# The input projection, the compression and both mixers of a transformer kernel laid out as one block on Trainium2

## The reference, cut to what matters

```python
a = rmsnorm(h, mix_norm[i])
proj = a @ w_in[i]
(hg_q, hg_f, hg_i, hg_g, n_q, n_kc, n_vc, n_ks, n_vs, n_kw, n_vw, n_gate) = jnp.split(proj, SPLIT_POINTS, axis=-1)
o_hg = hgrn2_mixer(hg_q, hg_f, hg_i, hg_g, lb_table[i], hg_out_norm[i])
o_nsa = nsa_mixer(n_q, n_kc, n_vc, n_ks, n_vs, n_kw, n_vw, n_gate, ...)
mixed = jnp.concatenate([o_hg, o_nsa], axis=-1).astype(h.dtype)
h = h + mixed @ w_out[i]
```

## Time and profile before

| | us |
|---|---|
| runs of the kernel before | 2066.91, 2068.8, 2072.6 |
| median | 2068.8 |
| the profiled execution: its own time | 2070.71 |
| its span in the trace | 2068.9 |
| PE busy in the span | 1998.7 |
| end of the last product of the projection | 98.4 |
| first instruction of the mixers on PE | 102.45 |
| last instruction of the mixers on DVE ends | 164.34 |
| first product of the output projection | 165.65 |

### The profile page before, as it was taken

One profiled execution on the slowest core, in us unless ns is written; L12 is line 12 of the kernel. 1 busy time (PEld: TensorE's weight loads), 2 busy tenths in 40 slices (PEclk: granted clock), 3 DMA queues, 4 the chain that ended last, 5 costly groups with the idle time before them and its releaser, 6 DMA issues. The chain is left out here.

```text
span 2068.9 us, 33672 instructions
## 1 busy us (share of the span) xinstructions
PE 1998.7 (97%) x13538; PEld 1761.6 (85%) x13538; DVE 1452.3 (70%) x2212; ACT 1058.8 (51%) x1977; POOL 34.5 (2%) x33
## 2 busy tenths in 40 slices
PE   8978999999999999999989999999999999998998
PEld 7868999999999888888877867877778888778998
DVE  7766599988898678888587757577764227667554
ACT  5664444467776555445573256452223217555444
POOL 0000000000000000000010000100000001000000
PEclk9989999999999999999999999999999999999999
DMA  6404556554444677777546420235673333124663
GB/s 240 150 1 130 176 184 186 190 166 135 146 138 145 197 253 262 257 254 251 163 133 206 161 72 17 92 133 186 240 280 108 102 99 101 32 73 154 194 190 126
DMA packets 94827, 326.90 MB, mean 158 GB/s; under 512 B 10321, under 2 KB 15825, under 8 KB 94673
## 3 DMA queue, kind: packets, MB, share of 16 engines
q1 hardware_dynamic: 94672, 324.75, 48.4%
HBM read 323.66 MB, written 1.05 MB: 157 GB/s over the span
## 5 line engine op out<-in xcount | busy, mean ns | idle before, releaser
L330 DVE TENSOR_TENSOR wlo<-raw,whi 128x1024 fp32r<-128x1024 f32 (+1 forms) x502 | 613.3, 1224 | 334.8 <-ACT whi L324 331.6
L324 ACT ACTIVATE whi<-raw 128x1024 fp32r<-128x1024 f32 (+1 forms) x502 | 525.4, 1049 | 378.2 <-PE ps L705 365.6
L703 PE MATMUL ps<-x_hi,whi 128*128 128x512 f32 (+1 forms) x976 | 333.1, 341 | 12.6 <-DVE x_lo L506 8.2
L704 PE MATMUL ps<-x_lo,whi 128*128 128x512 f32 (+1 forms) x976 | 329.1, 337 | 0.0
L705 PE MATMUL ps<-x_hi,wlo 128*128 128x512 f32 (+1 forms) x976 | 328.9, 337 | 0.0
L703 PE MATMUL ps<-xT_hi,whi 128*128 128x256 f32 x1136 | 324.7, 286 | 3.2 <-DVE xT_lo L504 2.9
L704 PE MATMUL ps<-xT_lo,whi 128*128 128x256 f32 x1136 | 318.3, 280 | 0.0
L705 PE MATMUL ps<-xT_hi,wlo 128*128 128x256 f32 x1136 | 316.7, 279 | 0.0
L703 PEld LDWEIGHTS ps<-x_hi,whi 128*128 128x128 f32 x976 | 183.4, 188 | 45.0 <-issue 14.3
L703 PEld LDWEIGHTS ps<-xT_hi,whi 128*128 128x128 f32 x1136 | 214.3, 189 | 3.5 <-issue 3.5
L704 PEld LDWEIGHTS ps<-xT_lo,whi 128*128 128x128 f32 x1136 | 214.5, 189 | 0.0
(11 more groups left out here) (435 smaller groups left out, 3311.5 us busy)
## 6 DMA issues: line engine op xcount, KB each, us to landing
raw<-peer_u_t SPq DMA_DIRECT2D x128, 512.0 KB, 3.5
raw<-peer_v_t SPq DMA_DIRECT2D x128, 512.0 KB, 4.0
raw<-ffn_in_t SPq DMA_DIRECT2D x88, 512.0 KB, 4.4
x<-ada_t SPq DMA_DIRECT2D x64, 512.0 KB, 4.5
raw<-ffn_out_t SPq DMA_DIRECT2D x44, 512.0 KB, 3.7
raw<-qkv_t SPq DMA_DIRECT2D x36, 512.0 KB, 4.1
gated<-ada_t SPq DMA_DIRECT2D x32, 512.0 KB, 5.7
raw<-w_in_t SPq DMA_DIRECT2D x24, 512.0 KB, 3.8
```

Of the source, the lines that this page charges most:

```text
L324: act.activation(whi[:, n % SPLIT, 0:w], raw[:, g % RAW, 0:w], ACT.Copy).then_inc(hi_done, 1)
L330: dve.tensor_tensor(wlo[:, n % SPLIT, 0:w], raw[:, g % RAW, 0:w], whi[:, n % SPLIT, 0:w].bitcast(F32), ALU.subtract).then_inc(lo_done, 1)
L703: pe.matmul(place, wh, xh, start=start, stop=False, skip_group_check=shared)
L704: pe.matmul(place, wh, xl, start=False, stop=False, skip_group_check=shared)
```

## The change

It has six parts.

1. **Order of the tiles.** The weights are packed, and taken, in another order: keys, forget logits, queries `nqk`, `qs`, the tall tile of 280, `gate`, and the tall tile of 512 (`hg_v`) last.
2. **Queries without norm.** The queries stay as the projection gives them. Eight small matmuls (L1326, two columns each) sum their squares by token; the root (`q_root`), its inverse (`q_rstd`) and root times slope (`q_slope`) are columns of one number per token. `bias` takes the slope from `q_slope`, then multiplies the maxima with `q_rstd` (L1558, one more DVE instruction per step); the exponentials take `q_rstd` as their scale, a pointer operand beside the bias, which was one already. The query gain goes into the gains of the keys. `compare_begin` gets one more multiplication.
3. **Tangents.** Silu, Sigmoid (but the first use of it and the forget logits) and the gelu are written with Tanh: `twice_silu` is one Tanh on ACT and one multiplication on DVE from PSUM, and the factor 2 goes into later constants. The order of ACT's instructions holds 14 table loads in this stretch before and 8 after.
4. **Decays and compression under earlier pieces.** `CMP_AT` goes from 13, 16, 19, 22 to 10, 11, 12, 13; the scan, the decays and the compression's second half come at w = 12 to 20; the compressed scores, which were part of the mixers, come at w = 21 to 24. The roots of the key heads, the query sums and the compressed keys come together at w = 18, their reciprocals and what follows at w = 18 and 19.
5. **One block.** The mixers' code becomes methods `end` that run behind w = 28 in the same block; `hg_turn` (the transpositions of `hg_begin`) runs behind piece 26 and `scores(0)` behind piece 27. The scores lie in banks 4 and 5. SBUF for the mixers is taken before the projection.
6. **Order of the end.** `hg_state(2)` stands behind `scores(5)`, `hg_give(0)` ahead of `scores(6)`, `hg_give(1)` ahead of `scores(7)`; before, they stood ahead of `scores(3)`, `scores(4)` and `scores(5)`.

Cut to its core:

```diff
-CMP_AT = [13 + 3 * m for m in range(2 * CMP_LEN * 64 // 1024)]
+CMP_AT = [10 + m for m in range(2 * CMP_LEN * 64 // 1024)]
...
-            def pe(self, pe, w):
-                if w == 5:
-                    pe.wait_ge(kon_loaded, 16)
-                    pe.wait_ge(heads_squared, 1)
-                    pe.matmul(ps[:, 4, :], k("ones64"), hn[:, 4:6, :].rearrange("p c t -> p (c t)"), start=True, stop=True).then_inc(heads_summed, 1)
-                if w == 9:
-                    pe.wait_ge(heads_squared, 2)
-                    for g in range(2):
-                        mm = pe.matmul(ps[:, 5 + g, :], k("ones64"), hn[:, 2 * g:2 * g + 2, :].rearrange("p c t -> p (c t)"), start=True, stop=True)
-                    mm.then_inc(heads_summed, 1)
-                if w in CMP_AT:
-                    self.window(pe, CMP_AT.index(w))
...
+                if w == 7:
+                    pe.wait_ge(kon_loaded, 16)
+                    pe.wait_ge(heads_squared, 1)
+                    pe.matmul(ps[:, 4, :], k("ones64"), hn[:, :, :].rearrange("p c t -> p (c t)"), start=True, stop=True).then_inc(heads_summed, 1)
...
+                if w == 15:
+                    pe.wait_ge(heads_squared, 2)
+                    for qb in range(TB):
+                        for c in range(NSA_G):
+                            at = 2 * (NSA_G * qb + c)
+                            mm = pe.matmul(ps[:, 6, at:at + 2], qsq[:, c, qb * P:qb * P + P], k("ones64", 0, P).rearrange("p (h n) -> p h n", h=2)[:, :, 0],
+                                           start=True, stop=True)
+                    mm.then_inc(heads_summed, 1)
...
+                if w == 17:
+                    pe.wait_ge(cmp_squared, 1)
+                    pe.matmul(ps[:, 5, 96:96 + N_CMP], k("ones64"), csq[:, :], start=True, stop=True).then_inc(cmp_summed, 1)
+                if w == 21:
+                    pe.wait_ge(values_spread, 1)
+                    pe.wait_ge(act_evacuated.h, act_evacuated.at(4))
+                    self.compare(pe)
+                if w == 26:
+                    self.hg_turn(pe)
+                if w == 27:
+                    self.scores(pe, 0)
+                if w == 28:
+                    self.end(pe)
+            def end(self, pe):
+                self.hg_scores(pe)
+                self.scores(pe, 1)
+                pe.wait_ge(act_evacuated.h, act_evacuated.at(10))
+                pe.wait_ge(dve_evacuated.h, dve_evacuated.at(8))
+                self.hg_state(pe, 0)
+                self.hg_state(pe, 1)
+                self.scores(pe, 2)
+                self.turn(pe, 0)
+                self.scores(pe, 3)
+                self.turn(pe, 1)
+                self.attend(pe, 0)
+                self.scores(pe, 4)
+                self.turn(pe, 2)
+                self.attend(pe, 1)
+                self.scores(pe, 5)
+                self.hg_state(pe, 2)
+                self.turn(pe, 3)
+                self.turn_compared(pe)
+                self.attend(pe, 2)
+                self.hg_give(pe, 0)
+                self.scores(pe, 6)
+                self.turn(pe, 4)
+                self.attend(pe, 3)
+                self.attend_compared(pe, 1)
+                self.hg_give(pe, 1)
+                self.scores(pe, 7)
+                self.turn(pe, 5)
+                self.attend(pe, 4)
...
+                for n in range(4):
+                    act.activation(part(pr[:, i % 3, :], i, n), part(sc[:, i % 2, :], i, n), ACT.Exp, bias=nm[:, i % 2, n:n + 1],
+                                   scale=qrstd[:, qb, c, n // 2:n // 2 + 1], accum_out=sums[:, i % 3, n:n + 1]).then_inc(nsa_exp, 1)
...
+                if w == 17:
+                    act.activation(tcond[:, :], v("cond", 0, 2 * C), ACT.Tanh, scale=0.5).then_inc(halved, 1)
+                    act.wait_ge(compressed, 1)
+                    act.activation(csq[:, :], ps[:, 5, 64:64 + N_CMP], ACT.Square).then_inc(cmp_squared, 1)
+                if w == 18:
+                    act.wait_ge(heads_summed, 2)
+                    act.activation(hn[:, :, :].rearrange("p c t -> p (c t)"), ps[:, 4, :], ACT.Sqrt, bias=eps[:, :], scale=1.0 / 64).then_inc(heads_root, 1)
+                    act.activation(flat(qroot), ps[:, 6, 0:2 * TB * NSA_G], ACT.Sqrt, bias=eps[:, :], scale=1.0 / 64).then_inc(heads_root, 1)
+                    act.wait_ge(cmp_summed, 1)
+                    act.activation(csq[:, :], ps[:, 5, 96:96 + N_CMP], ACT.Sqrt, bias=eps[:, :], scale=1.0 / 64).then_inc(cmp_root, 1)
...
+                    ins = dve.scalar_tensor_tensor(out=sc[:, i % 2, half * w:half * w + w].rearrange("p (a t) -> p a t", a=2),
+                                                   in0=dist[:, qb:qb + 1, 0:SEEN[i]].broadcast_to([P, 2, SEEN[i]]), scalar=qslope[:, qb, c, half:half + 1],
+                                                   in1=ps[:, SCORE_BANK + half, 0:w].rearrange("p (a t) -> p a t", a=2), op0=ALU.mult, op1=ALU.add)
+                ins.then_inc(nsa_biased, 1)
...
+                low = nm[:, i % 2, :].rearrange("p (h a) -> p h a", h=2)
+                dve.tensor_tensor(low, low, qrstd[:, qb, c, :].unsqueeze(2).broadcast_to([P, 2, 2]), ALU.mult).then_inc(nsa_max, 1)
+
...
+                if w == 18:
+                    dve.wait_ge(halved, 3)
+                    dve.tensor_scalar(tcond[:, :], tcond[:, :], 0.5, 0.5, ALU.mult, ALU.add).then_inc(curved, 1)
+                    dve.wait_ge(heads_root, 1)
+                    dve.reciprocal(hn[:, 0, :], hn[:, 0, :]).then_inc(heads_rstd, 1)
+                    dve.wait_ge(curved, 3)
+                    dve.tensor_tensor(v("cond", 0, 2 * C), v("cond", 0, 2 * C), tcond[:, :], ALU.mult)
+                    self.key_head(dve, 0)
+                if w == 19:
+                    dve.reciprocal(hn[:, 1, :], hn[:, 1, :]).then_inc(heads_rstd, 1)
+                    dve.wait_ge(heads_root, 2)
+                    dve.reciprocal(flat(qrstd), flat(qroot)).then_inc(heads_rstd, 1)
+                    dve.tensor_tensor(flat(qslope), flat(qroot), mk("slopes"), ALU.mult).then_inc(heads_rstd, 1)
+                    self.key_head(dve, 1)
+                    dve.wait_ge(cmp_root, 1)
+                    dve.reciprocal(crs[:, :], csq[:, :]).then_inc(heads_rstd, 1)
+                    dve.wait_ge(heads_rstd, 5)
+                    dve.scalar_tensor_tensor(out=kcn[:, :], in0=ps[:, 5, 64:64 + N_CMP], scalar=v("nsa_k", 0), in1=crs[:, :], op0=ALU.mult, op1=ALU.mult).then_inc(kcn_done, 1)
+                    dve.tensor_tensor(vblk[:, :, :], ps[:, 5, P:2 * P].unsqueeze(1).broadcast_to([P, NSA_G, P]),
+                                      k("rows").unsqueeze(2).broadcast_to([P, NSA_G, P]), ALU.mult).then_inc(values_spread, 1)
...
+        def twice_silu(n, dst):
+
+            return ("wide", n * P, slice(0, T), lambda act, place: act.activation(dst, place, ACT.Tanh, scale=0.5),
+                    lambda dve, place: dve.scalar_tensor_tensor(out=dst, in0=dst, scalar=1.0, in1=place, op0=ALU.add, op1=ALU.mult))
...
         product_stage(at_in, aH, [
             (4, 2, 512, [first(0), both(1, pair_of(cin, 0), ACT.Copy), first(2), dve_both(3, pair_of(nqk, 4))]),
+            (4, 2, 512, [first(0), both(1, pair_of(sig, 0), ACT.Sigmoid), first(2), both(3, pair_of(sig, 2), ACT.Sigmoid)]),
             (4, 2, 512, [first(0), both(1, pair_of(nqk, 0), ACT.Copy), first(2), dve_both(3, pair_of(nqk, 2))]),
-            (4, 2, 512, [first(0), both(1, pair_of(sig, 0), ACT.Sigmoid), first(2), both(3, pair_of(sig, 2), ACT.Sigmoid)]),
-            (4, 2, 512, [first(0), both(1, pair_of(qs, 0), ACT.Silu), first(2), both(3, pair_of(qs, 2), ACT.Silu)]),
-            (4, 2, 280, tall_n), (4, 2, 512, tall_v),
-            (4, 2, 512, [first(0), both(1, pair_of(gate, 0), ACT.Silu), first(2), both(3, pair_of(gate, 2), ACT.Silu)])],
+            (4, 2, 512, [first(0), twice_silu(1, pair_of(qs, 0)), first(2), twice_silu(3, pair_of(qs, 2))]),
+            (4, 2, 280, tall_n),
+            (4, 2, 512, [first(0), twice_silu(1, pair_of(gate, 0)), first(2), twice_silu(3, pair_of(gate, 2))]),
+            (4, 2, 512, tall_v)],
```

972 lines of the change are left out of this document (467 added, 505 removed).

## The result

The changed kernel takes **2076.68 us** (median of 8 runs, 2074.9 to 2080.81), the kernel before 2067.84 (8 runs, 2066.79 to 2072.6). The ratio is 1.0038, with a 95% interval of 1.0029 to 1.0047: 8.8 us slower by the medians and 7.9 by the ratio, which compares all runs; both are beyond the 6.2 us that the prediction named as the least that can be told from no change. Predicted were 2075.8, in a range of 2064 to 2085, with 0.52 on slower. Its profiled execution took 2076.37 us, with a span of 2074.6.

The account below looks back on a forecast made before the run. PE, busy 97% of the span, was taken to bound the kernel, with the mixers a chain over three engines. Terms 4.0 + 2.0 + 1.1 + 1.2 - 1.3 = +7.0 us on 2068.8 gave 2075.8, range 2064 to 2085.

Parts of the forecast that it names:

- Step 1, the projection: Projection: PE waits 2.35 and 2.95 us for late splits at pieces 19 and 20; with moved work, `bias(0)` starts 4.0 later.
- Step 2, the clock in the projection: Projection behind those waits: some 5 us of products run at half speed, +2.0 us taken.
- Step 1, what the one block is worth: End of the projection: the barrier's 2.40 us is saved, contained in the +4.0 by which `bias(0)` starts later.
- Step 3, the order of the mixers: Mixers from `bias(0)` on, at full clock: 5.7 us won up to `bias(5)`, 6.8 given back, +1.1.
- Step 4, the pointers: Mixers' 32 exponentials: a second pointer operand costs 0.04 us each, +1.2 us, bounds 0 to 2.2.
- Step 5, the low stretch that goes: Start of the mixers: the low-clock stretch up to 108 us goes, -1.3 us; the other 5.0 of low stretches stays.
- the first: Rival: PE never waits at pieces 19 and 20, total -0.3 us, 2068.5, no difference; chance 0.20.
- The clock did not stay up: Rival judged: clock at 1.00 through the mixers to the end, -6.5 us, 2062.3; chance 0.10.
- fall so much more often: Rival: clock falls again and again in projection and mixers, three further stretches add 6.0, +13 us, 2081.8; chance 0.20.

Follow-up runs that it names:

- x1_spread: Changed kernel with the DVE steps of w = 18 and 19 drawn apart and the compressed keys' square behind piece 18: 2070.92 us, +0.8 to the kernel before.
- x2: Changed kernel with `hg_state(2)` and both `hg_give` back where the kernel before has them in the mixers: 2074.49 us, +4.4 to before.
- x3: Changed kernel without the exponentials' scale pointer, `bias` slope a constant, queries' norm left out of the scores: 2072.56 us, +2.4 to before.
- y2: Changed kernel with only the mixers' order exchanged for a third one, scores one step further ahead: 2059.56 us, -9.2 to before.
- y3: Changed kernel with 16 idle transpositions ahead of the waits of `turn(0)`, `turn(2)`, `turn(6)` and 8 ahead of `turn_compared`: 2077.49 us, +8.8 to before.
- x7_spread_late_start: `x1_spread` with `hg_turn` and `scores(0)` behind the last piece, ACT's `hg_copies` moved from w = 27 to 28: 2071.76 us, +2.4 to before.
- The three experiments: Old order of the end on the changed kernel (2074.49 us) and on `x1_spread` (2071.1); new order of the end on the kernel before (2070.5).
- both experiments: Changed kernel without the second pointers (2072.56 us); kernel before with a pointer to ones as the exponentials' scale (2069.8 us).
- x6: `x1_spread` with a third order of the mixers, scores one step further ahead of `turn` and `attend`: 2054.82 us, -14.5 to before.
- y4_before_pointer: Kernel before with a pointer to a column of ones as scale of the 32 exponentials: 2069.8 us, +1.1 to before.

## Why the prediction was right, and where it was not

**Step 1, the projection: right in mechanism and size.** Forecast was PE waiting 2.35 and 2.95 us near 74 and 78; it waited 2.33 and 1.91, and the second one 2.64 at full clock. The root ended at 74.0 where 73.7 was laid out. Undoing the bunching took 8.0 us off the difference of medians, 6.2 by the ratios (`x1_spread`).

**Step 2, the clock behind the stalls: right.** +2.0 was taken from the row at 100 us; the granted clock was 0.73 and 0.50 from 76 to 84 us, and `bias(0)` came 6.0 us later, the sum of the two terms. `x1_spread` gave back 6.2. That the sum fits to a tenth is in part luck: the stretch behaves differently in each execution, and the four traces that hold the changed kernel's projection under another name (`x2`, `x3`, `y2`, `y3`) have `bias(0)` at 108.5, 110.2, 110.0 and 110.5.

**Step 1, what the one block is worth: the size right, the reason loose.** The sum had the barrier's 2.40 as saved and eaten by moved work. `x7_spread_late_start` shows the more exact reason: ACT's copies stand ahead of the last two splits and wait 4.92 us, so that what PE saves DVE loses.

**Step 3, the order of the mixers: +1.1 within what was found.** The three experiments put it at 0 to 3. The offsets laid out for full clock (22.2 for `bias(5)`, 30.4, 36.0) came as 26.3, 36.7 and 42.6; those of the kernel before (27.9, 33.8, 36.9) are 30.8, 36.8 and 40.0 in its trace. So the lead that the new order wins up to `bias(5)` and gives back came as forecast in kind, 4.5, 0.1 and -2.6 us where 5.7, 3.4 and 0.9 were laid out. The layout at full clock held none of the low stretches; that they make the whole difference is not shown.

**Step 4, the pointers: the term that was mis-sized.** I took 0.04 us for each exponential, below the 0.07 of the nearest row, and nothing for `bias`, whose slope becomes a pointer as well. Measured were 0.09 and, per `bias`, 0.12 for the pair. That is 3.0 + 1.0 us on the engines where 1.2 stood; how much of it reached the total is not shown (on the kernel before 1.1 us for the 3.0, in an interval from nothing to all of it). The Trainium skill, "ScalarE: Activation LUTs", section "What ACT_TABLE_LOAD costs", has about 93 ns for each [128,1] pointer operand; the traces of the changed kernel and of both experiments agree with it (0.585 against 0.49), and the page was nearer than my reading of one row.

**Step 5, the low stretch that goes: half right.** It went (1.00 at 108 to 116 us), but the others grew: in windows of 2 us the granted clock is 0.71 or less at 118 to 126, 132 to 136, 142 to 146 and 156 to 164 us, and before at 102 to 108, 114 to 118, 124 to 128 and 148 to 158. Over the mixers it is 0.83 in both. So the gain of 1.3 doesn't show, and step 4 was too small as well. Both would take the mixers over the forecast +1.0; together they would make more than the +2.0 of the trace, and no experiment parts them: the same mixers took 61.8, 62.9 and 62.0 us in the traces of the changed kernel, `x1` and `x7`.

**The rivals.** PE did wait, so the first falls; its price was right, since `x1_spread`, which makes it true, is at +0.8 (-0.2 to +3.7) where -0.3 was worked out. The clock did not stay up. Nor did it fall at each wait: before, PE waited 2.40 us ahead of 139.05, and the granted clock was 1.00 from there to 148 us. It did not fall so much more often than before that it cost 6 either. What no rival had was that the mixers' order held more than the whole change in either direction: I compared the two orders that were given and took the chain as it stood.

## What to carry to other kernels

- Steps that hang behind the pieces of a stream have a budget per piece (here 1.53 us for a narrow one, of which the split takes 0.74 on DVE). Ask for each engine what stands between two splits: ten instructions in two gaps, two long reciprocals among them, cost PE 4.2 us of waiting and a stretch of half clock, and the same instructions drawn apart 0.74.
- A chain over three engines with waits of 3 to 6 us was here a question of order before it was one of instruction cost. Laying it out by hand with measured durations and letting the scores run one step further ahead brought 9.5 us on the kernel before and, by the differences to before, 18.0 on the changed kernel (`y2`) and 15.3 on `x1_spread` (`x6`), more than any other single edit here.
- Work brought forward on one engine can be lost on another: here ACT's copies of it stood ahead of the last two splits, which the next stage needs. Look at what is queued behind the consumer.

## What the runs showed of the hardware that I had not expected

- A second pointer operand costs an ACTIVATE 0.09 us for 256 columns: an exponential follows the one before it after 0.49 us with one pointer and after 0.585 with two. The 0.07 that the prediction took for the first (0.42 and 0.49) compares a square with an exponential that also sums, and is no clean price.
- A pointer in place of an immediate (a constant in the instruction) costs a DVE scalar_tensor_tensor from PSUM 0.06 us (1.40 against 1.28 us for two).
- With 48 us of work in 60 instead of 42, PE's granted clock was 0.87 instead of 0.83 (`y3_after_filled`), and no time was won.
- The same products at the same granted clock are not always equally fast. From 300 to 500 us, in code that the change leaves alone, PE is full and at 1.00 in both traces, but a piece of 24 products takes 2.83 us before and 2.80 in the changed kernel. ACT takes a result out once per piece, first before, then in the changed kernel:

```profile
289.83 0.39 ACT L2063 ACTIVATE gated<-ps 128x256 f32<-128x256 f32 x1 [1.49 <-PE ps L705]
...
292.66 0.39 ACT L2063 ACTIVATE gated<-ps 128x256 f32<-128x256 f32 x1 [1.49 <-PE ps L705]
```

```profile
291.91 0.39 ACT L2115 ACTIVATE gated<-ps 128x256 f32<-128x256 f32 x1 [1.47 <-PE ps L706]
...
294.71 0.39 ACT L2115 ACTIVATE gated<-ps 128x256 f32<-128x256 f32 x1 [1.47 <-PE ps L706]
```

The 200 us hold 1711 records before, 1723 in the changed kernel, 1722 in `x1_spread` and 1710 in `x6_spread_new_order`, about 1.4 us of work more or less. `y4_before_pointer`, whose code there is that of before, has 2.80 us per piece. There is no pattern by kernel, and no run here tells the cause.
